# Hybrid decoder step, one core: adaLN rows get a place of their own, cache positions are interleaved over the partitions

## What is computed

```python
def trunk_layer(x, mod, g_mix, g_ffn, lp, past, ffn):
    sh1, sc1, gt1, sh2, sc2, gt2 = [m[:, None, :] for m in jnp.split(mod.astype(x.dtype), 6, axis=-1)]
    h = rmsnorm(x, g_mix) * (1 + sc1) + sh1
    y, state = token_mixers(h, lp, past)      # SSD | FoX attention | gated DeltaNet | MoBA, one in- and one out-projection
    x = x + gt1 * y
    h = rmsnorm(x, g_ffn) * (1 + sc2) + sh2
    x = x + gt2 * ffn(h)                      # dense in layer 0, 2 of 8 experts in layer 1
    return x, state
# mod = silu(c) @ w_ada[l] + b_ada[l]: 9 rows (one prompt, 8 sequences) of 6 * 1024 columns
# the sample tokens attend to 256 cached positions per sequence, in 2 pages of 128 from a pool (page_table)
```

## Time and profile before

| | us |
|---|---|
| median of 3 runs | 1509.15 |
| lowest, highest | 1504.14, 1519.63 |
| the profiled execution | 1509.24 |
| its span | 1507.3 |
| TensorE busy in it | 1346.8 |
| VectorE, ScalarE busy | 882.6, 642.2 |

### The profile page before, as it was taken

How to read it: one execution, slowest core, us unless ns; L and a number is a source line. 1 busy time by engine, 2 the same in 40 slices (tenths; PEclk the granted TensorE clock), 3 DMA queues, 4 the chain that set the end, 5 groups by cost and what they waited for, 6 DMA issues and landing times.

```text
span 1507.3 us, 24422 instructions
## 1 busy us (share of the span) xinstructions
PE 1346.8 (89%) x10071; PEld 1141.2 (76%) x10071; DVE 882.6 (59%) x1575; ACT 642.2 (43%) x1098; POOL 10.1 (1%) x22
## 2 busy tenths in 40 slices
PE   5999888859799998998878877899999999999995
PEld 3887755637799997887756555787978898898875
DVE  1140725541555554131624734799899988988996
ACT  2133212210444432233122201677676767767773
POOL 0000000000000000000000000000000000000000
PEclk9999967759899999999866688999999999999998
DMA  9539245695355354459036482489789889978991
GB/s 390 193 131 127 122 170 192 197 185 238 113 177 197 116 198 147 148 147 185 39 116 208 67 268 101 155 330 354 283 337 355 315 312 330 362 288 331 347 334 65
DMA packets 30327, 326.68 MB, mean 217 GB/s; under 512 B 6019, under 2 KB 6531, under 8 KB 8067
## 3 DMA queue, kind: packets, MB, share of 16 engines
q1 hardware_dynamic: 28738, 319.17, 63.2%
q0 software_dynamic: 1472, 5.89, 1.0%
HBM read 319.15 MB, written 5.89 MB: 216 GB/s over the span
## 4 chain that ended last, share of the span: by engine, by line
PE 78%; DVE 7%; DMA 6%; ACT 4%; issue 3%; SPq 2%; DVEq 0%; POOL 0%; ACTq 0%; POOLq 0%
PE bank L1100 15%; PE bank L1101 14%; PE bank L1102 14%; PE bank L725 12%; PE bank L1096 4%; DMA ring<-in_w_ada 4%; PE bank L767 2%; PE bank L640 2%; DMA ring<-in_cache_moba_v 1%; PE bank L1184 1%; SPq L544 1%; PE bank L617 1%; PE bank L663 1%; DMA out_gdn_p<-arena 1%; PE bank L672 1%
## 5 line engine op out<-in xcount | busy, mean ns | idle before, releaser
L2288 DVE TENSOR_TENSOR w_low<-ring,w_high 128x1024 fp32r<-128x1024 f32 x352 | 399.3, 1171 | 46.1 <-ACT w_high L1668 45.1
L1668 ACT ACTIVATE w_high<-ring 128x1024 fp32r<-128x1024 f32 x352 | 342.2, 1017 | 15.1 <-PE bank L1102 13.9
L725 PE MATMUL bank<-hT,ring 128*128 128x264 f32 x832 | 186.6, 386 | 0.0
L1100 PE MATMUL bank<-w_high,hcH 128*128 128x512 f32 x448 | 184.6, 412 | 2.2 <-DVE w_low L2288 1.8
L725 PEld LDWEIGHTS bank<-hT,ring 128*128 128x128 f32 x832 | 157.7, 190 | 26.9
L1102 PE MATMUL bank<-w_low,hcH 128*128 128x512 f32 x448 | 175.7, 392 | 0.0
L1101 PE MATMUL bank<-w_high,hcL 128*128 128x512 f32 x448 | 175.4, 392 | 0.0
L1346 ACT ACTIVATE arena<-bank 128x264 f32<-128x264 f32 (+8 forms) x128 | 51.7, 409 | 252.9 <-PE bank L725 84.5
L1100 PE MATMUL bank<-w_high,hidH 128*128 128x256 f32 x448 | 128.5, 287 | 3.0 <-DVE w_low L2288 3.0
L1101 PE MATMUL bank<-w_high,hidL 128*128 128x256 f32 x448 | 126.7, 283 | 0.0
L1102 PE MATMUL bank<-w_low,hidH 128*128 128x256 f32 x448 | 126.7, 283 | 0.0
(11 more groups left out here) (382 smaller groups left out, 2105.9 us busy)
## 6 DMA issues: line engine op xcount, KB each, us to landing
ring<-in_moe_gu SPq DMA_DIRECT2D x56, 2048.0 KB, 8.2
ring<-in_moe_down SPq DMA_DIRECT2D x32, 1792.0 KB, 7.3
ring<-in_w_ada SPq DMA_DIRECT2D x24, 2048.0 KB, 8.8
ring<-in_w_in SPq DMA_DIRECT2D x16, 1536.0 KB, 6.4
ring<-in_ffn_gu SPq DMA_DIRECT2D x11, 2048.0 KB, 7.9
ring<-in_ffn_down SPq DMA_DIRECT2D x8, 1408.0 KB, 6.0
ring<-in_w_out SPq DMA_DIRECT2D x4, 2048.0 KB, 24.9
ring<-in_cache_fox_k SPq DMA_DIRECT2D x32, 128.0 KB, 7.3
```

The lines of the kernel that those rows point to most:

```text
L725: ins = mm(b[:, 0:NT], w[:, k, m * P:(m + 1) * P], hT[:, k, :], start=k == 0, stop=k == KD - 1)
L1100: mm(out, wh, xh, start=start, stop=False)
L1668: A_(split(w_high), src, ACT.Copy).then_inc(sem("w_high_ready"), 1)
L2288: TT(split(w_low), src, split(w_high), ALU.subtract).then_inc(sem("w_low_ready"), 1)
```

## The change

The rows of an adaLN slab no longer go into its ring slot but into `mrow`, one 128x128 place of their own. An adaLN slab now gives one tick, behind its last product; the turn raises a semaphore of its own, `mod_turned`, on which `mod_columns` waits. The order of all instructions stays.

Sequence b now has partitions b, b+8, ..., b+120 (sixteen of them, each again with 8 neighbouring positions of a page); the loads, the masks and the reading order of the maximum follow.

```diff
@@ consts()
-    parts["later"] = (i[:, None] // SC == i[None, :] // SC) & (i[:, None] > i[None, :])
-    parts["own_col"] = (i[:, None] // SC == np.arange(NS)[None, :])
+    parts["later"] = (i[:, None] % NS == i[None, :] % NS) & (i[:, None] > i[None, :])
+    parts["own_col"] = (i[:, None] % NS == np.arange(NS)[None, :])
...
-    pos = slot // RUN * PAGE + (i[:, None] % SC) * RUN + slot % RUN
+    pos = slot // RUN * PAGE + (i[:, None] // NS) * RUN + slot % RUN
@@ plan_stream()
-    out = [("ada", 0, (c,), 2) for c in range(MIX_CHUNKS)]
+    out = [("ada", 0, (c,), 1) for c in range(MIX_CHUNKS)]
...
-        ada = [("ada", la, (c,), 2) for la, c in MIXER_ADA[l]]
+        ada = [("ada", la, (c,), 1) for la, c in MIXER_ADA[l]]
...
@@ build()
+        mrow = sb("mrow", [P, P])
@@ slab(i), keys and values; the gates alike
-                            sp.dma_start(r[b * SC:(b + 1) * SC, g * RUN * GW:(g + 1) * RUN * GW],
+                            sp.dma_start(r[b:P:NS, g * RUN * GW:(g + 1) * RUN * GW],
@@ ada_turn(l, c)
-                rows_ = ring[slot_of[index[("ada", l, c)]]]
-                tick(pe.transpose(b[:, 0:P], rows_[:, 0:P], C("ident")))
+                pe.transpose(b[:, 0:P], mrow[:, :], C("ident")).then_inc(sem("mod_turned"), 1)
@@ mod_rows(l, c), mod_columns(l, c)
-                copy(ring[slot_of[i]][:, 0:P], bank[0][:, 0:P], "mod_rows")
+                copy(mrow[:, :], bank[0][:, 0:P], "mod_rows")
...
-                act_e.wait_ge(tile_done, done_at[index[("ada", l, c)]])
+                o.need("mod_turned")
@@ the maximum over a sequence
-                vs(RED(ms8[0:8, :], bank[4][0:8, 0:P].rearrange("p (b c) -> p b c", b=NS), AX.X, ALU.max))
+                vs(RED(ms8[0:8, :], bank[4][0:8, 0:P].rearrange("p (c b) -> p b c", b=NS), AX.X, ALU.max))
```

More of the change, by code:

```diff
@@ L101, in consts @@
         parts[f"level{s}"] = (row // (2 * s) == colm // (2 * s)) & (row // s % 2 == 1) & (colm // s % 2 == 0)
-    parts["later"] = (i[:, None] // SC == i[None, :] // SC) & (i[:, None] > i[None, :])
-    parts["own_col"] = (i[:, None] // SC == np.arange(NS)[None, :])
+    parts["later"] = (i[:, None] % NS == i[None, :] % NS) & (i[:, None] > i[None, :])
+    parts["own_col"] = (i[:, None] % NS == np.arange(NS)[None, :])
     own_row = np.zeros((P, P))
-    own_row[:NS] = (np.arange(NS)[:, None] == i[None, :] // SC)
+    own_row[:NS] = (np.arange(NS)[:, None] == i[None, :] % NS)
     parts["own_row"] = own_row
-    parts["mates"] = (i[:, None] // SC == i[None, :] // SC)
+    parts["mates"] = (i[:, None] % NS == i[None, :] % NS)
     slot = np.arange(SP_)[None, :]
-    pos = slot // RUN * PAGE + (i[:, None] % SC) * RUN + slot % RUN
+    pos = slot // RUN * PAGE + (i[:, None] // NS) * RUN + slot % RUN
     sl = 2.0 ** (-8.0 * (np.arange(H) + 1) / H)
@@ L142, in plan_stream @@
 def plan_stream():
-    out = [("ada", 0, (c,), 2) for c in range(MIX_CHUNKS)]
+    out = [("ada", 0, (c,), 1) for c in range(MIX_CHUNKS)]
     for l in range(DEPTH):
         if l:
-            out += [("ada",) + (NORM_ADA["mix", l][0], (NORM_ADA["mix", l][1],), 2)]
+            out += [("ada",) + (NORM_ADA["mix", l][0], (NORM_ADA["mix", l][1],), 1)]
         out += [("in", l, s, s[1] // P) for s in IN_SLABS]
-        ada = [("ada", la, (c,), 2) for la, c in MIXER_ADA[l]]
+        ada = [("ada", la, (c,), 1) for la, c in MIXER_ADA[l]]
         out += [("k", l, (m,), 0) for m in range(2)] + ada + [("v", l, (m,), 1) for m in range(2)]
@@ L152, in plan_stream @@
         if l == 0:
-            out += [("ada",) + (NORM_ADA["ffn", l][0], (NORM_ADA["ffn", l][1],), 2)]
+            out += [("ada",) + (NORM_ADA["ffn", l][0], (NORM_ADA["ffn", l][1],), 1)]
             out += [("gu", l, (c,), 4) for c in range(FF // 256)]
@@ L577, in _ @@
                             for g in range(PAGES):
-                                load(lf[b * SC:(b + 1) * SC, g * RUN:(g + 1) * RUN, :],
+                                load(lf[b:P:NS, g * RUN:(g + 1) * RUN, :],
                                      A["cache_fox_logf"][l].rearrange("n (c s) h -> n c s h", s=RUN)[
```

## The result

| | before | after |
|---|---|---|
| median of the runs, us | 1514.39 (4 runs, 1504.14 to 1524.19) | 1464.03 (4 runs, 1459.74 to 1465.01) |
| ratio after to before | | 0.966, 95% interval 0.959 to 0.974 |
| span of the profiled execution, us | 1507.3 | 1458.0 |
| TensorE busy in it, us | 1346.8 | 1319.4 |
| what is left of the span, us | 160.5 | 138.6 |

The fourth and fifth line of the table say where to look: of the 49.3 us between the two profiled executions TensorE's idle time gives 21.9, and 27.4 are **the same instructions taking less time on TensorE**. That second part was no term of the sum.

A forecast was written before the change was run, and what follows sets the result against it. TensorE was taken to hold 78% of the chain, so gains come where the chain leaves it, largely for late loads. Terms of 16.9 us (layer 0) and 9.9 (layer 1), less 0.2, gave 26.6: 1509.2 to 1482.6 us, range 1472 to 1494.

The forecast's parts named there:

- The store's race: Before the SSD phase: GDN state store no longer shares DMA with a slab load; 2.8 us in layer 0, 3.5 in layer 1.
- a6, a8, b5, b7: adaLN slabs in attention, a for layer 0, b for layer 1: waits of 2.65, 3.64, 2.49 and 2.94 us go.
- The bound on a7: Layer 0 attention: slab a7 might land late; 0.4 us taken back for a7 and a8 together, bounds 0 and 1.2.
- A new wait at a7 nearly as long as the old ones: Sign of being wrong: a new wait at slab a7 or a8 in layer 0's attention, as long as the old ones.
- The values: Cached-value products: earlier loads remove TensorE's wait, 8.2 us in layer 0 and 1.0 in layer 1.
- Interleave: Cache loads on every eighth partition: issue unchanged at 8.38 us for 16, no cost or gain beyond the values' waits.
- Loss by slower loads: Rival: strided cache loads at, say, 60 GB/s make values and keys late, giving 1572 us; chance 0.03.
- Maximum: Maximum over a sequence, 0.28 us, reads its values strided; 0.2 us in all taken as cost.
- TensorE's clock moves: Rival: taking out idle lifts or sinks TensorE's clock; 1473 us up (chance 0.11), 1494 us down (0.09).
- units at 1.95 or 3.64 us in other proportion than now: Sign of being wrong: adaLN units of 64 products split differently between 1.95 us (2.4 GHz) and 3.64 us (1.2 GHz).

The follow-up runs named there:

- Kernel 5: Kernel after, but loads into the ring slots of slabs a1, a2, b1 and b2 wait for those slabs' turns again; 1472.1 us.
- kernel 9: Kernel after with the old order of cache positions and the cached-value loads waiting for the adaLN slab's turn again; 1481.8 us.
- 10: Kernel after, interleaved positions kept, with only the cached-value loads waiting for the adaLN slab's turn again; 1461.8 us.
- kernel 3: Kernel after with the interleave undone, so sequences lie on 16 neighbouring partitions and only the own place for adaLN rows remains; 1468.7 us.
- kernel 6: Kernel before with 65 unused products filling TensorE's waits for a6, a8, b5, b7 and the cached values, no transfer moved; 1495.4 us.
- 7: Kernel after with unused products ahead of the share waits of attention steps 3 and 6 and ahead of a7 and b6; 1454.4 us.
- 12: Kernel after with unused products only ahead of the share waits of attention steps 3 and 6, in both layers; 1457.8 us.

## Why the prediction was wrong, step by step

As waits, the terms of the sum were borne out, with one exception (a7 and its neighbours). What failed is the term that the sum put at nothing: TensorE's work was to take as long as before, and the clock stood only among the rivals, sized too small and given too little chance.

1. **The store's race.** Forecast 2.8 us in layer 0, 3.5 in layer 1. The wait fell from 14.5 to 6.3 us in all (landings of 6.51 and 7.15 us, became 2.3 and 3.1, not quite the 1.8 of the earlier trace rows); from 200 us (201.5 after, for the program starts 1.4 us later) to a4 it took 11.4 us instead of 14.3, 2.9 less. In layer 1 the exponential L1512 came 6.5 us after the store was sent instead of 10.4, 4.0 less. Kernel 5 gives 4.3 to 6.0 us back to the rest of the span against 6.3 forecast. Right.
2. **a6, a8, b5, b7.** Their waits (2.65, 3.64, 2.49, 2.94) are gone, but for 0.27 at a8 and 0.31 at b7. Right.
3. **The bound on a7.** 0.4 us were taken for a7 and a8 together, with 1.2 as the upper bound, and nothing for b6 and b7. Measured 2.33 at a7, 0.27 at a8, 1.20 at b6, 0.31 at b7: 4.1 us. The term took a landing of 7.70 to 9.39 us from the earlier trace rows and the distances of units at 1.2 GHz. Both moved: a6 follows a5 4.6 us later instead of 7.8, so the loads of a7 and a8 leave at 238.9 and 241.9 us, run side by side, and take 8.7 and 12.5 us to land. At a7 the distance shrank from the 8.7 us of the forecast to 6.5, and that is the wait; most of it is a6's unit at the higher clock. The mechanism was named, its size was off by 3.7 us in all. A new wait at a7 nearly as long as the old ones was one of the prediction's own signs of being wrong.
4. **The values.** Forecast 9.2 us; kernels 9 and 10 put the wait by itself at 9.8. Right as a wait. Its removal is worth 13 to 20 us (kernel 9 against 3, after and 10).
5. **Interleave.** Taken at no cost and no gain beyond the values: kernel 3 agrees. The DMA engines moved 209 GB/s from 110 to 135 us, around the keys' loads, instead of 121 to 123, each load landing in 2.9 us. Issue was not unchanged, as the prediction had it: 16 loads took 10.8 and 10.0 us to issue. The estimate from the Trainium skill, "SBUF — State Buffer", section on the DMA port swizzle, was about 19 us for a pair of slabs. That was near, but for another reason: issuing the pair alone took 20.9 us, from 275.77 to 296.66, and the last load landed 2.3 us later. Loss by slower loads: excluded.
6. **Maximum.** It takes 0.28 us as before; 0.2 us were taken for nothing.

So the waits that went are 26.6 less 3.7, about 23 us, and TensorE's idle time fell by 21.9. This part of the sum holds.

**The step that failed** is the clock's: the sum left it out, and the rival "TensorE's clock moves" had it as "Up: eight units at 1.6 us each would be 13, of which the two-slot loop of loads passes some 9", with the chance 0.11 against 0.09 for down and the sentence "Nothing in the rows says which". It priced the adaLN units alone. Measured: 0.915 to 0.932 in the mean of the timed executions, 17 us by the line above; 27.4 us of TensorE's busy time in the two profiled ones, of which up to 11 is the spread between executions of one kernel. The two readings leave 17 to 27 us for the clock, and 22 to 29 for the waits, which together make the 46 to 50. In the rows, some 10 us of it stand at the waits that went: 6.3 in the units a6, a8, b5 and b7, and about 4 in the value products and w_out (28.8 us after, 30.1 and 30.2 before), which the rival had not counted. For the rest no run shows which wait, if any, it belongs to.

Could the rows have said it? Only half. The four units behind the waits that were to go ran at or near the lower level (3.62 and 3.24 us in the earlier trace rows, b5 and b7 at 3.64 in the earlier trace rows), and that was the hint; but b3 behind a wait of 1.83 us ran high, and of the six units without a wait in the earlier trace rows four ran low (a4, a5, a7, a10). Its own sign of being wrong, "units at 1.95 or 3.64 us in other proportion than now", came: 4 of the 18 units in the mixers took 1.95 or 1.96 us before, 10 after. Only a run like kernel 6, which leaves the wait and takes the idleness, tells a cause from a companion.

What stays open: how far the clock falls by waits and how far by small products. Kernel 6 shows that work set into a wait holds it up, and 7 and 12 make it likely; but from 195.2 to 202.9 us in the kernel before, in the GDN chain and the unit behind it, it stands at 0.50 with TensorE busy for 7.7 of 7.7 us, and no run took those products away.

## What to carry to other kernels

Price a wait on TensorE at its own length and then look at what stands behind it: if the next products run at 1.2 GHz, the wait that goes takes part of their time with it (here 9.8 us of waiting were worth 13 to 20). Before reading a gain from one profiled execution, look at a stretch that the change leaves alone in two executions of the same kernel (here 20.2 and 15.6 us). When units speed up, the distances from which a load's slack was read shrink with them, so slack has to be counted again at the higher clock. Before moving independent work out of a wait to where another engine is late, see which wait it covers where it stands.

## What the runs showed of the hardware

- Useless products set into waits made the kernel before 14.1 us faster and the kernel after, by medians, 6 to 10 us; more of them ahead of the inversion, the SSD products and w_out won nothing.
- TensorE was busy for 7.7 of 7.7 us, from 195.2 to 202.9 in the kernel before, at a granted clock of 0.50: a full busy share did not go with the higher level.
- Executions of one kernel differ by their granted clock, on one chip too: 0.900 to 0.922 over 42 of the kernel before on four chips, with 24 us between the ends; 0.900 to 0.921 and 18 us on one of them.
- Sixteen-partition loads of 128 KB landed in a median of 2.8 to 2.9 us with a stride of eight partitions, and of 7.3 to 15.1 us on sixteen neighbours, where one queued behind the other. Their issue got slower: 10.8 us for 16 instead of 8.4, so the queue, not the transfer, set the pace of the pair.
- A 64 KB store took 6.5 to 7.2 us beside a 2 MB slab load and 2.3 and 3.1 after, where none was on its way but in the last 0.7 us of the second.
